# Last layer: the modulation products ahead of the output products, and another order of ten weight slots

## The reference, cut to what matters

```python
m = (sc @ w_ada[i] + b_ada[i]).reshape(bsz, 1, N_MOD, D_MODEL)      # six modulation rows
...
y_lat = o_l.reshape(bsz, t, MLA_OUT) @ w_out                          # output products
x = x + m[:, :, 2] * y_lat
h_lat = modulate(rmsnorm(x, norm_ffn[i]), m[:, :, 3], m[:, :, 4])
x = x + m[:, :, 5] * ec_moe(h_lat, ...)

def ec_moe(h, w_router, w_gate, w_up, w_down):
    aff = softmax(h @ w_router)
    gates, idx = lax.top_k(jnp.swapaxes(aff, 1, 2), cap)              # 64 tokens for each expert
    xs = h[idx]
    a = xs @ w_gate[e];  u = xs @ w_up[e]
    y = (silu(a) * u) @ w_down[e] * gates                             # added back at idx
```

## The kernel before

| in turn | gate 0 | up 0 | modulation 5 | gate 1 | down 0 | up 1 |
|---|---|---|---|---|---|---|
| slots before (h0, h1) | 4, 5 | 0, 1 | 6, 2 | 3, 11 | 9, 6 | 2, 10 |

## Time and profile before

### The profile page before, as it was taken

One profiled execution on the slowest core, in us unless ns is written; L12 is line 12 of the kernel. 1 busy time (PEld: TensorE's weight loads), 2 busy tenths in 40 slices (PEclk: granted clock), 3 DMA queues, 4 the chain that ended last, 5 costly groups with the idle time before them and its releaser, 6 DMA issues.

```text
span 2513.5 us, 26492 instructions
## 1 busy us (share of the span) xinstructions
PE 2221.0 (88%) x10170; PEld 1254.1 (50%) x10170; DVE 1297.7 (52%) x2310; ACT 980.2 (39%) x1609; POOL 479.0 (19%) x512
## 2 busy tenths in 40 slices
PE   6998998999888986999999997779999788777787
PEld 2444544446666444666766674446665333222222
DVE  2147526436875147889888985366662411111111
ACT  2024323114555035887888783355552100000000
POOL 0000000000134111356545620042321000000000
PEclk9999999999999997999999999889999889999999
DMA  7122611101000358999999997400032699999998
GB/s 279 67 71 92 226 48 38 67 17 68 1 1 2 135 217 300 359 369 373 366 377 368 374 361 288 171 11 1 1 132 105 245 384 409 406 406 405 405 412 337
DMA packets 92426, 546.29 MB, mean 217 GB/s; under 512 B 7791, under 2 KB 10623, under 8 KB 67598
## 3 DMA queue, kind: packets, MB, share of 16 engines
q1 hardware_dynamic: 84750, 521.02, 53.1%
q0 software_dynamic: 6144, 20.98, 3.6%
q10 hardware_dynamic: 1408, 2.62, 0.3%
HBM read 523.62 MB, written 20.97 MB: 217 GB/s over the span
## 4 chain that ended last, share of the span: by engine, by line
PE 23%; DMA 15%; DVE 12%; ACT 6%; issue 4%; POOL 1%; another core or an unknown queue 0%; SPq 0%; ACTq 0%; POOLq 0%; DVEq 0%
DMA AR<-in_w_exp_up_dram 8%; DVE RW L2087 8%; PE PS L2121 5%; PE PS L2336 5%; DMA AR<-in_w_exp_down_dram 4%; PE PS L684 3%; ACT AR L2175 3%; ACT RW L2079 2%; PE PS L985 2%; PE PS L898 2%; DMA AR<-in_w_exp_gate_dram 2%; PE PS L695 2%; PE PS L2530 1%; DVE AR L2294 1%; PE PS L2682 1%
## 5 line engine op out<-in xcount | busy, mean ns | idle before, releaser
L2087 DVE TENSOR_TENSOR RW<-AR,RW 128x2048 fp32r<-128x2048 f32 x192 | 432.3, 2283 | 45.7 <-ACT RW L2079 45.7
L2336 PE MATMUL PS<-AR 128*64 128x512 f32 x1536 | 370.9, 631 | 86.0 <-DMA AR<-in_w_exp_gate_dram 41.8
L2079 ACT CAST RW<-AR 128x2048 fp32r<-128x2048 f32 x192 | 364.7, 1916 | 120.1 <-PE PS L2121 106.5
L2121 PE MATMUL PS<-RW,RX 128*96 128x512 f32 x1536 | 362.9, 395 | 4.5 <-DVE RX L2227 4.0
L2121 PEld LDWEIGHTS PS<-RW,RX 128*96 128x96 f32 x1536 | 247.8, 162 | 110.7 <-issue 5.2
L2336 PEld LDWEIGHTS PS<-AR 128*64 128x64 f32 x1536 | 114.0, 144 | 317.4 <-issue 254.1
L2121 PE MATMUL PS<-RW,RA 128*96 128x512 f32 x768 | 186.3, 399 | 12.3 <-DVE RA L2284 12.3
L1713 PE MATMUL PS<-AR 128*128 128x512 f32 (+1 forms) x480 | 190.1, 552 | 0.7 <-ACT AR L620 0.7
L684 PE MATMUL PS<-AR 96*128 96x512 f32 (+3 forms) x480 | 183.8, 500 | 3.7 <-POOL AR L661 2.3
L784 DVE TENSOR_REDUCE AR<-PS 128x1 f32<-128x768 f32 (+1 forms) x160 | 135.9, 849 | 97.3 <-PE PS L684 79.0
L2413 POOL DMA_INDIRECT x_rows<-AR x16 | 119.0, 7439 | 332.2 <-DVE AR L2294 244.9
(11 more groups left out here) (346 smaller groups left out, 2685.3 us busy)
## 6 DMA issues: line engine op xcount, KB each, us to landing
AR<-in_w_exp_gate_dram SPq DMA_DIRECT2D x64, 2048.0 KB, 14.7
AR<-in_w_exp_up_dram SPq DMA_DIRECT2D x64, 2048.0 KB, 12.4
AR<-in_w_exp_down_dram SPq DMA_DIRECT2D x64, 2048.0 KB, 14.0
AR<-in_w_ada_dram SPq DMA_DIRECT2D x30, 2048.0 KB, 11.9
AR<-in_w_in_dram SPq DMA_DIRECT2D x6, 2048.0 KB, 9.3
AR<-in_w_in_even_dram SPq DMA_DIRECT2D x4, 2048.0 KB, 7.8
AR<-in_w_out_dram SPq DMA_DIRECT2D x2, 2048.0 KB, 8.1
AR<-in_w_out_even_dram SPq DMA_DIRECT2D x2, 2048.0 KB, 7.6
```

The lines of the kernel that those rows point to most:

```text
L2079: s.copy(pair(i)[0], raw_half(key, hf)).then_inc(*S.up("hi", l, i))
L2087: v.tensor_tensor(lo, raw_half(key, hf), hi.bitcast(F32), ALU.subtract).then_inc(*V.up("split", key, hf))
L2121: m = pe.matmul(bank(ob)[0:Mc, :], st_, mv[:, k, 512 * q_:512 * q_ + 512], start=(k0 + k == 0 and n_ == 0), stop=(k0 + k == 7 and n_ == 2))
L2336: m = pe.matmul(bank(b)[64 * q_:64 * q_ + 64, :], op, w[:, c, 512 * q_:512 * q_ + 512], start=(h == 0 and c == 0), stop=(h == 1 and c == 3 ...
```

## The change

Three edits. The order of the ten slots is another, and modulation 5 goes to slots 2 and 0. PE computes the four products of modulation 3 and 4 of the last layer ahead of the output products. VectorE copies the two rows of modulation 3 ahead of its part of the output products. The first layer's order stays.

| in turn | gate 0 | up 0 | modulation 5 | gate 1 | down 0 | up 1 |
|---|---|---|---|---|---|---|
| slots after (h0, h1) | 4, 5 | 3, 6 | 2, 0 | 1, 11 | 2, 0 | 9, 10 |

```diff
-        two, four, ten = [0, 1], [0, 1, 2, 6], [4, 5, 0, 1, 3, 11, 9, 6, 2, 10]
+        two, four, ten = [0, 1], [0, 1, 2, 6], [4, 5, 3, 6, 1, 11, 2, 0, 9, 10]
...
                 if (nm, l, e, h) == ("gate", 1, 1, 0):
-                    ada_loads(1, [5], [6, 2])
+                    ada_loads(1, [5], [2, 0])
...
         def dve_moe(l):
             tag = f"m{l}"
-            for h in range(2):
+            for h in range(2 if l == 0 else 0):
                 dve_ada_row(l, 3, h)
...
-        def pe_moe(l):
+        def pe_ada_products(l):
             for j, b0 in ((3, 6), (4, 4)):
                 for h in range(2):
                     pe_ada_mm(l, j, h, b0 + h)
+
+        def pe_moe(l):
+            if l == 0:
+                pe_ada_products(l)
             pe_ada_end(l, 3, 6, 7)
...
             pe_pairs(ATO, lambda it: pe_up(it[1], it[2]))
+            pe_ada_products(1)
             P.wait_ge("read", "pv", "o", 63)
             pe_outproj("outo", None, OT4)
...
             dve_pairs(ATO, lambda it: dve_up(it[1], it[2]))
+            dve_ada_row(1, 3, 0)
+            dve_ada_row(1, 3, 1)
             dve_outproj("outo", OT4, None, tmps, 1)
```

## The result

The changed kernel takes 2522.97 us (median of 11 runs, 2518.39 to 2527.97) against 2515.91 us of the kernel before beside it (11 runs, 2512.89 to 2518.94). The ratio is 1.0026, 95% interval 1.0018 to 1.0034: slower by 6.5 us, between 4.5 and 8.6. The same kernel once more, beside other runs of the kernel before, gave 1.0017 (1.0006 to 1.0028). The likeliest case of the prediction was a loss of 3 us, which would have passed for no change. On the prediction's scale (2515.61 us before) the ratio is 2522.2 us: inside its range of 2512.0 to 2522.5, close to the upper end, and above the forecast's own 2514.2 to 2520.6.

The account below looks back on a forecast made before the run. The prediction took the weight stream to bound the kernel, through its restart and gate 0's release. Release 11.1 us later against 8.7 gained, plus 0.6, gave +3.0 us: 2518.6 us, range 2512.0 to 2522.5.

Parts of the forecast that it names:

- What bounds the kernel: Weight stream to the end: held first by slots under output weights, then by gate 0's release of its slots.
- Three transfers into the hole, a fourth held by slot 0: DMA's idle stretch during output products: three transfers, 15.6 us, move in; modulation 5's second half waits for output weights.
- (a): Fourth modulation product, ahead of the output products: PE waits for its weights, output products start 9.2 us later.
- (b): After that wait PE may have fallen to its low clock: +1.6 us, or 0 if it holds.
- (c): Behind the output products: of 7.0 us of products moved away only 1.2 leave the chain, -1.2 us.
- (d): PE's idle stretch between the modulations' transposes: low clock slows 28 transposes, +2.2 us, from +1.2 to +4.6.
- (e): The last layer's first gather gets shorter: -0.7 us, from -1.9 to +1.6.
- The restart: Gate 2 on an idle queue: second half lands 13.7 us after release, 22.4 before; break-even 8.7 us.
- The net: Release 11.1 us later against 8.7 us of gain: +2.4; with another +0.6, +3.0 us, from -1.4 to +7.7.
- the term "+0.6": Behind the stream's restart: one gather of 64 rows, 0.65 us of DMA, now falls there, +0.6 us.
- the slower rival: From output products to top-k PE's clock stays low: release 13.5 us later, end 5.4 later, 2521.0 us; chance 0.22.
- the sign of being wrong that I had named: After the restart: a stream at another rate than 403 GB/s, where 1% is already 4.6 us.

Follow-up runs that it names:

- order-only kernel: The kernel before with only the new order of slots, the modulation products staying behind the output products: ratio 1.0028.
- 6 us delay: The kernel before with expert 0's eight transposes done seven times over: ratio 1.0001.
- 14 us delay: The kernel before with expert 0's eight transposes done fifteen times over: ratio 1.0018.
- kept-warm kernel: The changed kernel with PE repeating a product and transposes in its two waits: ratio 1.0010 to the kernel before.
- two ahead: The kernel before with only modulation 3's two products and both row copies ahead, other slots: 0.9972; with products added to keep PE busy, 0.9969.
- slot 1 first: The kernel before with slots 0 and 1 of the ten exchanged, so up 0's first half takes slot 1: ratio 0.9987.
- one ahead: The kernel before with only the first modulation product ahead of the output products, and another order of slots: ratio 0.9974.
- three ahead: The changed kernel with the fourth modulation product put back behind the output products: ratio 0.9990 to the kernel before.

## Why the prediction was right or wrong

*What bounds the kernel: right.* The order-only kernel (restart later, release unmoved), the 6 us delay (release later, free) and the 14 us delay (release later, counts) move one side at a time and come out so.

*Three transfers into the hole, a fourth held by slot 0: right.* SP's rows show it to the instruction. The queue then ran dry at about 2036, where I had 2032 and some us for the gathers.

*(a) and (b), the fourth product: right in kind, 1.4 us short in this profile, 0.5 too dear in the other.* The output products ended at T0 + 67.85 against 55.63: +12.2, where I had 9.2 + 1.6 = 10.8. Its weights took 9.3 us to land and not 7.9. The clock fell in the 3.5 us wait; against the kept-warm kernel the fourth product took 0.6 us longer (2.49 to 1.92) and the output products 1.1 (56.28 to 55.20), which is the 1.6 of (b). In the second profile of the changed kernel (b) was 0, the other value that I had named; which of the two an execution gets, the rows could not say.

*(c) and (d), behind the output products: right in their sum.* From their end to the conversion of the indices behind the top-k (line 2036) it was 38.5 us (2010.37 - 1971.87) and is 38.85 (2023.50 - 1984.65): +0.35 (+1.3 in the second profile), where I had -1.2 + 2.2 = +1.0.

*(e): right within its bounds.* The gather took 10.0 us and not 10.6, and 12.1 in the second profile.

*Not in my sum:* gate 0's first half. From PE's start on the experts to the release it was 5.45 us and is 6.53 (5.64 and 5.93 in the second profiles): the low clock of the gather wait lasted on for longer. With two ahead and PE kept busy it is 3.7. I had taken gate 0's duration as fixed.

*The restart: 1.1 us too dear.* I took 13.7 us from release to landing, from a pair issued 0.4 us apart. Gate 2's second half goes 3.4 us behind the first, when gate 0's second half has been used, as the earlier trace rows already showed, and then takes 9.2 us. In all seven profiles in which the queue had run dry it is 12.4 to 13.1 (changed kernel 12.6). So the break-even is 22.4 - 12.6 = 9.8 us of release and not 8.7.

*The net:* 13.1 - 9.8 = +3.3 us at the landing, measured; I had 11.1 - 8.7 = +2.4. Two errors near cancelled, which was luck. (The range's lower end, -1.4, also leaves out the 0.6 that the sum adds.)

*Where it failed: the term "+0.6" for what lies behind the restart.* Between the landing and the last scatter the changed kernel loses another 3.2 us in the first pair of profiles and 2.0 in the second. With it the last scatter is 6.4 and 5.7 us later, past the 0.2% that I took for no change; without it, it isn't. (By the ratios it is past 0.2% in the first set of runs, 1.0026, and not in the second, 1.0017.) So the case that came is between my forecast and the slower rival, and by neither's mechanism alone: the clock did rise again under the transposes, so the rival's place was wrong.

What these 2 to 3 us are is open; where they stand is not. The four profiles that keep the old order and a full queue take 456.1 to 457.4 us for that stretch. The three with a new order and a full queue (order only, slot 1 first, one ahead) take 458.5 to 458.6, the one with the old order and a queue run dry (14 us delay) 458.8, those with both 457.8 to 460.3. So a part may be the order of slots and a part the restart from nothing; with one profile of most kernels I can't part them. The order-only kernel's rival, a loss that builds up over the experts, is not what the traces show. From the landing to the fourth of the sixteen scatters the kernel before takes 82.5 and 83.2 us in its two profiles, the changed one 84.6 and 84.9; the twelve scatters behind take 373.6 and 373.8 against 374.6 and 374.1. So 1.7 to 2.1 of the 2.0 to 3.2 us are lost in the first 85 us. The DMA rate agrees: 406 and 403 GB/s before against 401 and 400 in these 85 us, and 406 to 407 in all four in the 365 us behind them. So the sign of being wrong that I had named, a stream at another rate after the restart, shows only there. The order isn't the main part of the result: three ahead has the changed kernel's order and is 9 us faster than it.

By the Trainium skill's rule on transposes (TensorE: Matmul & The Clock Gate, Part 4: PE-mode transpose) the clock would have stayed low through the routing. The trace differs for those of 128 by 128: in the changed kernel the clock was back at 0.96 in the stretch after 1995.2, and ahead of the first routing product at 1997.34 PE had done nothing but transposes. For those of 64 by 64 (last section) it agrees.

```profile
1991.60:1995.20 3.60, 3.57 (x17) 3.60 (x18) 2.43 (x10) 0.16 (x1) 0.00 (x0) 0.50 1.11 451
1995.20:2000.00 4.80, 4.37 (x33) 3.21 (x31) 2.18 (x4) 2.33 (x3) 0.00 (x0) 0.96 0.93 347
```

## What to carry to other kernels

A prefetch stream has two ends: when it can start, and when its first slot comes back. Work out the backlog at the first release; that is all that an earlier start can win, and any delay of the consumer is paid out of it. Moving work ahead to free a slot is worth it only for work whose own operands are already there: two products with landed weights gained 7 us, three gained 2.5 (not clear of noise), and the fourth, whose weights were still to come, made it a loss of 6.5 (the orders of slots differ between the first and the other two). And where a delay leaves PE idle, count the low clock that can follow too, at the wait and again at the next stage; with a wait near 3 us, as here, count it as a chance: it came after 3.54 us, and after 2.68 in the earlier trace rows, and not after 3.25.

## What the runs showed of the hardware that was not expected

In the 14 us delay PE did 120 transposes of 64 by 64 back to back, and the granted clock stayed at 0.50 (1.2 GHz) through all 14.6 us, where I had expected it to rise. PE in order of time, then the stretches:

```profile
2021.47 14.63 PE L2314 MATMUL PS<-AR 64*128 64x64 f32 x120 [3.51 <-DMA AR<-h_rows,AR]
```

```profile
2021.50:2025.00 3.50, 3.50 (x30) 3.50 (x30) 0.00 (x0) 0.00 (x0) 0.00 (x0) 0.50 0.98 293
2025.00:2029.00 4.00, 4.00 (x36) 4.00 (x35) 0.00 (x0) 0.00 (x0) 0.00 (x0) 0.50 1.04 321
2029.00:2033.00 4.00, 4.00 (x36) 4.00 (x35) 0.00 (x0) 0.00 (x0) 0.00 (x0) 0.50 0.98 395
2033.00:2036.00 3.00, 3.00 (x26) 2.92 (x25) 0.00 (x0) 0.00 (x0) 0.00 (x0) 0.50 1.00 426
```

It had risen while PE did 48 transposes of 128 by 128, and in two ahead with PE kept busy it was at 1.00 after the first three of the added products, which followed two others of their size. Why the small ones left it low no run here tells.

The issue of a small transfer can hold SP for long: the 8 KB bias row took 15.39 us to issue with six transfers of 2048 KB not yet landed, and 0.38 us in two ahead, where one was. Here nothing behind it could have gone anyway.

A gather of 64 rows of 4 KB took about 10 us from issue to landing whether the stream's queue had a backlog or was running out: the last layer's first one 9.6 to 10.6 us in thirteen of the fourteen profiles (10.0 in the changed kernel, 10.6 in the kernel before), and 12.1 in the changed kernel's second.
